# A float32 decoder trunk on one core: attention by half units in the order A, B, D, C, and a setup that multiplies feature tile by feature tile

## What is computed

```
mod = silu(c) @ w_ada[l] + b_ada[l]            # 6 x 1024 numbers: shift, scale, gate, twice
h   = rms_norm(x) * gain1 * (1 + scale1) + shift1
cols = h @ w_in[l]    # q,k,v of A, B, C; forget logits and gate of C; latents and index keys of D
A: softmax(q1 k1) - lam * softmax(q2 k2), times v, sub-norm      (4 heads, 8 maps)
B: softmax(q k + bias) v                                          (4 maps)
C: softmax(q k + cumulative log forget gates) v, times a gate     (4 maps)
D: latents -> q, k, v; an indexer keeps the 64 best keys of each query; softmax v   (4 maps)
x  = x + gate1 * (concat(A, B, C, D) @ w_out[l])
h  = rms_norm(x) * gain2 * (1 + scale2) + shift2
x  = x + gate2 * ((silu(conv(h @ w_gate)) * conv(h @ w_value)) @ w_down)
```

## Time and profile before

| | |
|---|---|
| median of three runs | 793.75 us |
| the profiled execution | 795.83 us, its span 794.1 us |
| PE busy | 738.2 us, 93% of the span |
| DVE, ACT, POOL busy | 498.3, 395.2, 125.3 us |
| PE's share of the chain that ended last | 78% |
| mean granted PE clock | 0.975 |

### The profile page before, as it was taken

The page is one execution under the profiler, slowest core; times in us unless marked ns, Lnnn a source line. Parts: engine busy times, 40 slices in busy tenths (PEclk is TensorE's granted clock), DMA queues, the critical chain, the costliest instruction groups (busy, mean ns, idle before and its releaser), DMA issues.

```text
span 794.1 us, 14962 instructions
## 1 busy us (share of the span) xinstructions
PE 738.2 (93%) x6249; PEld 690.4 (87%) x6249; DVE 498.3 (63%) x876; ACT 395.2 (50%) x633; POOL 125.3 (16%) x91
## 2 busy tenths in 40 slices
PE   4888789979999999999999999988899999999996
PEld 2577779968899999999998878977888999999996
DVE  1271367663578887979756456775467676756674
ACT  2252754442465746565545665443446445454442
POOL 1000100030402464536300010012120000000001
PEclk9599999999999999999999999999999999999998
DMA  9999986660429685868963786683045545555501
GB/s 295 343 304 240 301 285 211 212 197 18 160 64 308 213 267 171 285 217 267 322 185 115 228 269 213 213 257 115 4 156 177 194 162 200 171 189 183 177 36 54
DMA packets 139543, 158.37 MB, mean 199 GB/s; under 512 B 4931, under 2 KB 133076, under 8 KB 139476
## 3 DMA queue, kind: packets, MB, share of 16 engines
q1 hardware_dynamic: 139476, 157.41, 61.8%
HBM read 155.76 MB, written 1.64 MB: 198 GB/s over the span
## 4 chain that ended last, share of the span: by engine, by line
PE 78%; DVE 5%; ACT 4%; issue 1%; DVEq 0%; ACTq 0%
PE bank L787 22%; PE bank L788 21%; PE bank L789 21%; PE bank L801 3%; DVE w_lo L1410 2%; PE bank L1090 2%; ACT w_hi L1179 1%; PE bank L841 1%; PE bank L1103 1%; ACT work L1326 1%; PE bank L1102 1%; PE bank L1101 1%; PE bank L986 1%; PE bank L817 1%; PE bank L984 1%
## 5 line engine op out<-in xcount | busy, mean ns | idle before, releaser
L787 PE MATMUL bank<-act_hi,w_hi 128*128 128x256 f32 (+1 forms) x1040 | 299.3, 288 | 6.7 <-DVE w_lo L1410 3.2
L1410 DVE TENSOR_TENSOR w_lo<-raw,w_hi 128x2048 fp32r<-128x2048 f32 (+1 forms) x98 | 234.6, 2395 | 111.0 <-ACT w_hi L1179 110.9
L788 PE MATMUL bank<-act_lo,w_hi 128*128 128x256 f32 (+1 forms) x1040 | 295.2, 284 | 0.0
L789 PE MATMUL bank<-act_hi,w_lo 128*128 128x256 f32 (+1 forms) x1040 | 295.0, 284 | 0.0
L1179 ACT ACTIVATE w_hi<-raw 128x2048 fp32r<-128x2048 f32 (+1 forms) x98 | 184.8, 1889 | 154.7 <-PE bank L789 144.6
L787 PEld LDWEIGHTS bank<-act_hi,w_hi 128*128 128x128 f32 (+1 forms) x1040 | 199.5, 192 | 14.4 <-issue 11.8
L788 PEld LDWEIGHTS bank<-act_lo,w_hi 128*128 128x128 f32 (+1 forms) x1040 | 199.7, 192 | 0.1
L789 PEld LDWEIGHTS bank<-act_hi,w_lo 128*128 128x128 f32 (+1 forms) x1040 | 199.6, 192 | 0.0
L787 PE MATMUL bank<-mlp_hi,w_hi 128*128 128x256 f32 x352 | 100.0, 284 | 5.5 <-DVE mod L1445 3.1
L788 PE MATMUL bank<-mlp_lo,w_hi 128*128 128x256 f32 x352 | 99.6, 283 | 0.0
L789 PE MATMUL bank<-mlp_hi,w_lo 128*128 128x256 f32 x352 | 99.6, 283 | 0.0
(11 more groups left out here) (179 smaller groups left out, 881.6 us busy)
## 6 DMA issues: line engine op xcount, KB each, us to landing
direct<-in_w_ada SPq DMA_DIRECT2D x48, 1024.0 KB, 10.1
raw<-in_w_ffn_up SPq DMA_DIRECT2D x44, 1024.0 KB, 5.1
raw<-in_w_in SPq DMA_DIRECT2D x22, 1024.0 KB, 6.7
raw<-in_w_ffn_down SPq DMA_DIRECT2D x22, 1024.0 KB, 5.0
raw<-in_w_out SPq DMA_DIRECT2D x8, 1024.0 KB, 5.3
bias<-toeplitz SPq DMA_DIRECT2D x4, 384.0 KB, 11.3
heads_out<-in_x SPq DMA_DIRECT2D x1, 1024.0 KB, 8.8
out<-heads_out SPq DMA_DIRECT2D x2, 512.0 KB, 3.1
```

Of the source, the lines that this page charges most:

```text
L787: pe.matmul(dst, lh, rh, start=first, stop=False, skip_group_check=check)
L788: pe.matmul(dst, lh, rl, start=False, stop=False, skip_group_check=check)
L789: return pe.matmul(dst, ll, rh, start=False, stop=last, skip_group_check=check)
L1410: nc.vector.tensor_tensor(w_lo[n % RAW][:, s], raw[n % RAW][:, s], w_hi[n % RAW][:, s].bitcast(F32), ALU.subtract).then_inc(lo_done, 1)
```

## The change

- `MAPS` runs A, B, D, C. `TURNS` and `OUT_K` turn the groups and multiply the rows of w_out in that order. D's biases have a tile of their own, `chosen_bias`, which POOL fills for all four heads right after the last `choose`. The first turned group goes into `mlp_hi` and `mlp_lo`.
- `maps(2)` is called after half a unit in several places, beginning with the first half of unit 5. Ten calls take the 20 scores, the last after the first half of unit 11. w_in's pairs in layer 0 move from units 2 and 3 to places between halves, the last one among the w_out units. Index products, relu and latents use other buffers. `scores` and `values` gain waits on `in_read`.
- The last w_out unit is preceded by pieces 3 to 8 of unit 14 in place of 6 to 8.
- In the setup the adaLN tiles come as (0, 4), (1, 5), (2, 6), (3, 7), each pair shift and scale of two feature tiles, and each is scaled, rounded and multiplied by units 0, 1 and 2 before the next. x is loaded first; units 0 and 1 ahead of tile 2 of the list, unit 2 ahead of the last pair, units 3 and 4 right behind it. The bias table is expanded after the third pair.
- The MLP's wait for the second gap pair moves into the first down product, ahead of its column tile 4.

```diff
-MAPS = [(0, h, c) for h in range(4) for c in range(2)] + [(g, h, 0) for g in (1, 2, 3) for h in range(4)]
+MAPS = [(0, h, c) for h in range(4) for c in range(2)] + [(g, h, 0) for g in (1, 3, 2) for h in range(4)]
+TURNS = [0, 1, 3, 2]
+OUT_K = [k for g in TURNS for k in (2 * g, 2 * g + 1)]
+def pair_units(l, u):
+
+    return (u // 2, u // 2 + SETUP_ADA // 2) if l == 0 and u < SETUP_ADA else (u, u + 1)
...
+    if l == 0:
+        s += [("unit", 0, 6, KT), ("evac", 0), ("split_hi", 3), ("unit", 1, 6, KT), ("evac", 1), ("unit", 2, 6, KT),
+              ("evac", 2), ("narrow", 0), ("split_lo", 3), ("latents_norm", 0), ("split_hi", 4), ("split_lo", 4),
+              ("forget", 0), ("unit", 3, 0, KT), ("evac", 3), ("latents", 0), ("split_hi", 5), ("split_lo", 5)]
...
+    split(7)
+    first_half(5)
+    maps(2)
+    second_half(5)
+    s.append(("split_hi", 8))
+    maps(2)
+    s.append(("split_lo", 8))
+    choice()
+    first_half(6)
+    pair()
+    choice()
+    second_half(6)
+    pair_turn()
+    s.append(("split_hi", 9))
+    maps(2)
+    s.append(("split_lo", 9))
+    choice()
+    first_half(7)
+    if l == 0:
+        pair()
+    maps(2)
+    choice()
+    second_half(7)
...
+    first_half(11)
+    maps(2)
     s.append(("turn", 0))
...
+    second_half(11)
+    s.append(("split_hi", NI + 2))
+    s += [("probs", m) for m in scored]
+    s += [("unit", NI, 0, 2), ("turn", 1), ("split_lo", NI + 2)]
+    values(turned)
+    s += [("unit", NI + 1, 0, 2), ("turn", 2)]
+    values(scored)
+    pair()
+    s += [("unit", NI, 2, 4), ("unit", NI + 1, 2, 4)]
+    pair_turn()
+    s += [("unit", NI, 4, 6), ("turn", 3), ("unit", NI + 1, 4, 6), ("unit", NI + 2, 0, 3)]
+    for i, k0 in ((NI, 6), (NI + 1, 6), (NI + 2, 3), (NI + 3, 0)):
...
+            pe.wait_ge(cond_ready, 1)
+            ada_half(0, 0, 0, 0)
+            mean_of(0)
+            ada_half(0, 0, 1, 0)
+            spread(0)
...
+            pe.wait_ge(vec_in, 5)
+            first_units(0, 2)
             ada_turn(0, 2)
-            mean_of(0)
             ada(0, 4)
+            first_units(2, 4)
+            ada_turn(0, 4)
+            pe.wait_ge(table_in, 16 * 2)
+            pe.wait_ge(tab_ready, 1)
+            pe.matmul(bank[4][0:3 * HEADS, 0:384], tab[:, :], buck[:, :], start=True, stop=True).then_inc(diag_up, 1)
+            unit_product(0, 2, bank[2], None, 0, 2)
+            first_units(4, 6)
             ada(0, 6)
-            ada_turn(0, 4)
+            unit_product(0, 2, bank[2], None, 2, 4)
             ada_turn(0, 6)
...
+                        if j == 0 and ct == 4:
+                            pe.wait_ge(mod_ready, turned[0])
...
+            modulated(0, 0, 0, 4, 6)
+            act.wait_ge(diag_up, 1)
+            nc.scalar.activation(diag[:, :], bank[4][0:3 * HEADS, 0:384], ACT.Copy, scale=-1.0).then_inc(diag_ready, 1)
+            split_hi(2, unit_width(2))
+            take_rows(0, 6)
+            modulated(0, 0, 0, 6, KT)
```

More of the change, by code:

```diff
@@ L138, in layer_schedule @@
     pairs = [("pair", l, u) for u in range(PAIR_FROM[l], PAIR_TO, 2)]
-    early, late = (pairs[:2], pairs[2:]) if l == 0 else ([], pairs)
+    late = list(pairs)
     gap = GAP_PAIRS.get(2 * l, [])
-    turning = []
     choose = [("choose", r) for r in range(TOPK // 8)]
@@ L166, in maps @@
         nonlocal scored, turned
-        for m in scored:
-            s.append(("probs", m))
+        s.extend(("probs", m) for m in scored)
         values(turned)
@@ L176, in maps @@
             s.append(("softmax", m))
[L178 to L186, removed]
@@ L209, in layer_schedule, with split @@
-    s.append(("turn", 0))
[L210 to L225, removed]
+    def split(i):
+        s.extend([("split_hi", i), ("split_lo", i)])
@@ new lines, in first_half, with second_half @@
+    def first_half(i):
+        s.append(("unit", i, 0, KT // 2))
+    def second_half(i):
+        s.extend([("unit", i, KT // 2, KT), ("evac", i)])
+    if l:
+        split(6)
+    first_half(4)
+    if l == 0:
+        s.append(("latents_up", 0))
+        split(6)
+    second_half(4)
+    s += [("index", 0), ("index", 1), ("forget_up", 0), ("index", 2), ("index", 3)]
+    split(7)
[5 more added lines that the diff above has]
+    s.append(("split_lo", 8))
@@ new lines, in layer_schedule @@
+    maps(2)
+    s.append(("split_lo", 11))
+    choice()
+    choice()
+    first_half(9)
+    pair()
+    second_half(9)
+    pair_turn()
+    s.append(("split_hi", NI))
+    maps(2)
+    s.append(("split_lo", NI))
+    first_half(10)
+    if l == 0:
+        pair()
+    maps(2)
+    second_half(10)
+    if l == 0:
+        pair_turn()
+    s.append(("split_hi", NI + 1))
+    maps(2)
+    s.append(("split_lo", NI + 1))
+    first_half(11)
+    maps(2)
+    s.append(("turn", 0))
+    second_half(11)
@@ new lines, in layer_schedule @@
+    s.append(("split_hi", NI + 2))
[4 more added lines that the diff above has]
+    values(scored)
+    pair()
+    s += [("unit", NI, 2, 4), ("unit", NI + 1, 2, 4)]
+    pair_turn()
+    s += [("unit", NI, 4, 6), ("turn", 3), ("unit", NI + 1, 4, 6), ("unit", NI + 2, 0, 3)]
+    assert not late and not choose and at[0] == NM
+    for i, k0 in ((NI, 6), (NI + 1, 6), (NI + 2, 3), (NI + 3, 0)):
+        s.append(("unit", i, k0, KT))
@@ L979, in scores @@
                             pe.wait_ge(low_ready, 2 * (NM * l + m - 2) + 2)
+                        if part == 0 and g < 3:
+                            pe.wait_ge(in_read, NI * l + 3 * g + 5)
                         p0, width = ((h % 2) * HEAD + comp * HALF, HALF) if g == 0 else ((h % 2) * HEAD, HEAD)
```

270 lines of the change are left out of this document (145 added, 125 removed).

## The result

The kernel after took a median of 769.38 us over four runs (767.26 to 772.77), the kernel before beside it 795.32 (792.2 to 802.41, four runs): a ratio of 0.9666, 95% interval 0.9588 to 0.9744. The profiled execution took 767.26 us against 795.83, its span is 765.5 us and its mean granted clock 0.977, against 0.975. The same kernel measured a second time took 766.8 (ratio 0.9611, 0.9574 to 0.9647).

What follows compares the result with a forecast made beforehand. PE, busy 738.2 of 794.1 us, was taken as the bound. Setup 2.5, attention 11.1 and MLP 3.1 made 16.7, called 16.8: profile 795.83 to 779.0, median 777.0; forecast's own range 772 to 783, overall range 767 to 791.

Steps and rivals of the forecast that it cites:

- Setup, in time: Up to unit 5: new wait before unit 2, two pairs moved later, unit 5 starting at 86.2; 2.5 us gained.
- the waits of 3.09 and 1.40 go: At layer 0's forget gates: PE's two waits vanish because ACT no longer stands before unit 5's load.
- Attention: Both layers from unit 5: old waits and low clock go, new waits come; 5.7 and 5.4 us gained.
- the new waits: Softmax calls in attention: 2.5 us at the first call, 2.5 together after three `heads` steps; 5.0 a layer, bounds 1.5 and 9.
- MLP: First down product: 24 products ahead of the moved wait cover its 1.56 us; 3.1 us gained.
- theory A: Set up after the measurement for the 12 us lacking: the new attention order leaves fewer waits than counted.
- C: Set up after the measurement for the 12 us lacking: the setup is worth more than 2.5 us.
- B: Set up after the measurement for the 12 us lacking: the clock, falling behind waits, gave back more than they cost.
- The setup fills its waits: Rival, setup: ready work fills PE's waits, up to 10 of 12 us; 768 with attention waits at 4; chance 0.20.
- The slower rival: Attention: half units don't cover the exponentials, 2.9 us at each of 14 calls, 41 for 10; 808 us; chance 0.10.
- the setup pays more: Rival, setup: half clock from 35 to 61 costs 8 us; 785, or 789 with more attention waits; chance 0.20.
- The moves don't act: Rival, MLP: the wait only passes to column tile 4, 3.1 us come back; 780, inside the forecast's own range.

Runs made afterwards that it cites:

- the part alone: The kernel after with only the MLP's wait put back ahead of the first down product: 770.06 us, ratio 0.9652 against 0.9611.
- one edit of PE's order: The kernel after with tiles 4 and 5 of units 0 and 1 and the last adaLN pair ahead of unit 2 on PE: 762.88 us, ratio 0.9544.

## Why the prediction was right, and where it was not

The median of 769.38 lies in the range of 767 to 791, but with 2.4 us to spare, and the repeat at 766.8 lies 0.2 below it: that the number came inside was in part luck. The gain was 1.7 times the forecast. The mechanisms hold: PE's idle time falls where the prediction says, and the wait that it saw coming before unit 2 is there. By its own steps, from profile to profile:

**Setup, in time: close, and booked to one cause where there are two.** Predicted were a wait of 6.4 before unit 2 (6.01), unit 3 at 63.7 (61.94), and 21.0 us of idle time to unit 5 (20.6). Unit 5 starts at 83.0 in place of 86.2: 1.8 of it up to unit 3, 1.4 in the 21.1 us from there, taken as 22.5. So 5.7 us lie ahead of unit 5 in place of 2.5. But the step "the waits of 3.09 and 1.40 go, because unit 5's load is no longer what ACT stands before" names the new loads alone. In the old setup under the new attention the 4.5 us are already 2.5, at the index products, with ACT still before that load; so the new order takes 2.0 of them, and the new loads the rest. The new loads under the old attention leave 0.43 at the forget gates, though PE has waited 2.65 before that for the tiles of a pair. The new setup pays for what its loads save with its own waits of 6.01 and 1.97; by itself it saves no idle time, and somewhere from nothing to 8 us.

**Two index products: counted once too often.** They take 0.9 us. In the kernel before they stand behind unit 5, in the kernel after ahead of it:

```profile
101.62 0.50 PE L1059 MATMUL bank<-kiT,qiT 64*128 64x128 f32 x4
```

The prediction has them in its 22.5 us from unit 3 to unit 5, and so in the 2.5 gained, but does not give them back in the attention. Its sum is 0.9 short for that.

**Half clock: not twice.** The prediction takes products at 0.50 as twice as long. They take 0.21 us in place of 0.12, 1.8 times; by an estimate from its 38 products at that clock, its setup is about 1 us too long for it.

**Table load: on neither chain.** I took 1.0 us on the path. Unit 0's bank was ready only as the load ended: its last product ends at 56.97, and the copy at 57.23 starts 0.1 us behind the load. The Trainium skill, "ScalarE: Activation LUTs", section "What ACT_TABLE_LOAD costs", has 2.66 us with a drain of 1.38; the rows show the load at 1.28 us and the next activation 0.01 later, at 55.83. At 87.51 the time behind the load is 1.27 us of waiting for DVE's minimum.

**Attention: right in kind, too small by one term.** From unit 5 to the norm, and without the 0.9 us of index products, layer 0 gave 10.8 us in place of 5.7 (118.4 us became 111.8, with 5.1 us of pairs more in it), layer 1 gave 6.3 in place of 5.4 (118.0 became 110.8), with 6.8 us at 0.50 in it. The term that failed is the new waits, 5.0 a layer: they came to 1.5 and 2.0. The first call costs 1.5 where I had 2.5. The step "after a `heads` step DVE adds 1.6 before its softmax: 0.7 to 1.2, at three places 2.5 together" has waits of 0.33 and 0.21 in layer 1 and none in layer 0. The rows show why, DVE's first and then PE's, at B's `heads` in layer 0:

```profile
148.26 0.19 DVE L1707 RECIPROCAL rinv<-rsum 128x8 f32<-128x8 f32 x1
148.49 0.69 DVE L1713 TENSOR_TENSOR heads_out<-bank,rinv 128x512 f32<-128x512 f32 x1
149.22 0.15 DVE L1729 COPY rinv<-rinv 128x1 f32<-128x1 f32 x1
149.37 0.29 DVE L1692 CUSTOM_DVE_ANT_0 work<-bank,chosen_bias 128x128 f32<-128x128 f32 x1
```

```profile
148.28 0.49 PE L1072 MATMUL bank<-qkT 64*128 64x128 f32 x4
148.61 0.60 PE L1074 MATMUL bank<-qkT 64*128 64x256 f32 x4
149.14 0.39 PE L863 MATMUL bank<-act_hi,w_hi 128*128 128x256 f32 x1
...
152.56 0.49 PE L1178 MATMUL bank<-ident,work 128*128 128x128 f32 x3
```

`heads` begins as the last `values` ends, and that is when PE starts the new scores; it takes 1.1 us, 0.9 of them beside the scores, so that the softmax is 0.2 late. I had put the whole of it behind the scores. The half unit then covers the rest, and PE turns the probabilities at 152.56 without a wait.

**MLP: right.** 3.1 predicted, 3.3 measured with the part alone.

**The balance.** From the profile before to the one after, the idle time without the last 10 us of the span falls by 21.0 us (50.1 to 29.1) where the steps have 14.2 (3.4 in the setup, 7.7, 3.1): the 6.8 more are the waits just named, 3.5 and 3.0, and 0.4 in the setup. The clock gives 3.1 (31.4 us at 0.50 become 24.3), where the steps have 3.4. The index products are 0.9. The other 4.5 us are PE's own busy time at full clock, which the sum had not. It has a likely source, not tested: the last matmul before a wait is 0.28 long where the next would start after 0.12, and PE stood still 42 times before and 19 times after, 23 x 0.16 = 3.7. The stages agree roughly with the kernel after again: up to layer 0's second norm 15 waits fewer (2.4) go with 2.9 us, in layer 1's attention 4 fewer (0.6) with 1.0. 16.7 + 6.8 - 0.3 + 0.9 + 4.5 is 28.6. So of the 12 us that the prediction lacks, theory A has the largest part, C has 0.4 of idle time, and B has nothing between these two profiles. Beside that the clock matters more than the sum has it: in the run without half units it costs twice what the waits do, and over many executions the old attention costs 24 to 27 us for 16 to 18 us of idle time.

**Rivals.** "The setup fills its waits" gave 768 (10 us in the setup and 1 a layer under 777.0 are 765), close to the time measured, but for another reason: the wait of 6 us is there. It took one edit of PE's order to make it true. The slower rival fell by the half units. Against "the setup pays more" speaks that in both profiles of the kernel after the clock was at 0.50 up to 47.4 only, in place of 61; five other runs with the same setup have 3.4 us more of it near 62. "The moves don't act" fell by the MLP's wait, which did not pass on.

## What to carry to other kernels

Where every engine walks one list, let half a unit of ready matmuls lie between a product whose result other engines must work on and the step that reads it back: here an order built on this, with other parts beside it, took 16 to 18 us of waits out of two layers, and the time fell by 24 to 27; without the half unit at three calls a layer, 24 came back. Price a recurring wait above its length (1.5 times in that case, nearly 3 times in the run without half units), and compare versions by idle time first, since single low-clock stretches move between executions. When a moved step frees a wait, run that move without the rest: the earlier loads, which seemed to be the whole reason here, were only part of it.

## What was not expected of the hardware

The same program had its low-clock stretches in different places from one execution to the next: at 453.6 for 6.8 us in one profile, at 197.5 and 402.3 in the other, with equal waits. The places are not any places, though. The 13 profiles (of 12 kernels) pass 39 norms from layer 0's second to layer 1's second, and behind 22 of them a stretch at 0.50 begins 3.0 to 4.0 us after the norm's first matmul, 3.4 us long in 20 cases and 6.8 in two. The profiles show no wait of PE in these 3 to 4 us in any of the 22 cases. In the kernel after again:

```profile
194.06 1.39 PE L917 MATMUL bank<-mean_w,work 128*128 128x1 f32 x12
```

```profile
197.50:201.00 3.50, 3.50 (x28) 1.79 (x28) 0.75 (x3) 0.10 (x1) 0.71 (x1) 0.51 0.18 71
```

Each stretch of 3.4 us costs about 1.5, so the three norms alone can set two executions of one program over 4 us apart. The other 16 low stretches between 70 and 740 us all lie at a wait of PE or within 2.2 us behind one. Why a norm has its stretch in one execution and not in the next was not tested.

The Trainium skill, "TensorE: Matmul & The Clock Gate", section "HAM oscillation", has groups of matmuls between recurring waits begin at the lower clock. The kernel without half units agrees in kind, with five stretches at 0.50, 34.0 us long together, at its softmax waits of 1.6 to 2.3 us and none at the one of 1.03; the kernel after, with waits of 1.1 and 0.36 us at the same call, shows it in layer 1 of one profile and in no layer of the other. That waits behind unit 11 brought 3.4 us at 0.50 in the kernel before and 10.2 in the one with its attention order and the new setup is left open: the waits are nearly the same, and both are single profiles.
